# Sums of weight blocks made by adding transfers, and a seventh block product made from high and low digits

## The chip, the cores and the metric

The kernel runs on one core of a Trainium2 chip. The time is that of one execution on the device in microseconds, from the runs of the compiled program; the profile is that of one further execution.

## What is computed

256 tokens of width 1024 in float32 go through two layers of a first network and then through a tail of two more blocks. Each of the four has a mixer (sparse attention beside retention; stick-breaking attention beside a state-space model; attention over the best 64 keys) and an MLP with squared ReLU and 4096 hidden units. The change is in the four MLPs alone:

```python
# the two layers of the first network
h = rmsnorm(x, norm_mlp[i])
x = x + jnp.square(jax.nn.relu(h @ w_ff1[i])) @ w_ff2[i]
# the tail, MLPs "A." and "B."
return jnp.square(jax.nn.relu(x @ w1)) @ w2
```

## The kernel before

**Digits.** A float32 product on TensorE is replaced by three products of operands rounded to a shorter type: `products` multiplies low by high, high by low and high by high. ScalarE makes the high digits (a copy that rounds), VectorE the low ones (value minus high).

**Weights.** They come in tiles of 2 MB, loaded by SyncE (SP) into a ring of three slots. SP waits until TensorE has given back a slot (`tile_used`) and then issues the next load. In an MLP the tiles alternate: `ff1.n` holds 512 columns of the first matrix, `ff2.n` 512 rows of the second. The load of `ff2.n` goes to the slot of `ff1.n`, and so is issued when TensorE has finished with that.

**Seven products.** Of the eight `ff2` tiles the first seven (n = 0 to 6, `LAST` = 7) are not multiplied block by block (two token halves by two row halves by two column halves, eight products) but by a scheme with seven products. It needs sums of blocks of the hidden values (`dve_hidden_sums`, in `work`) and four sums of blocks of the weights: with b11, b12, b21, b22 the four blocks of a tile, `dve_form_sums` makes b22 - b12 into `t_sums[0]`, b12 - b11 in place in the ring's slot, b22 minus that into `t_sums[1]`, and b21 minus that into `t_sums[2]`. Six of the products are made by digits. The seventh, into bank 6, is the original float32 product of hidden values and `t_sums[2]`, two instructions of 512 columns a tile.

**One period**, the same for n = 2 to 7 in each MLP, on TensorE: unit (n, 0), which is eight times three products for each of two column blocks of `ff1.n` into bank 0; `seven_first(n-1)`, six products with the left columns' digits; unit (n, 1), again into bank 0; the slot of `ff1.n` is given back; `seven_second` and `seven_rest(n-1)`: left columns, bank 5 and bank 7 (right columns), bank 3 (`t_hi[0]`), bank 2 (`t_hi[1]`), bank 6. `form_used` counts four points of it: left columns' high digits read, right columns' read, bank 3 done, bank 2 done. Whoever writes into the buffers of the next tile waits for the count that frees them (`form_free`).

On ScalarE, in program order (`act_mlp_seven`): ReLU of unit (n, 0), square, high digits, half of `ff1.(n+1)`'s digits, ReLU of unit (n, 1) and the same again, digits of the hidden sums, then `act_column_forms(n)` and `act_right_forms(n)` for tile `ff2.n`, and after those the ReLU of unit (n+1, 0). For n = 1 this ReLU stands inside `act_right_forms` (`between`), behind the first cast. TensorE's unit (n+1, 1) waits for that ReLU, since it writes the same bank.

VectorE makes the low digits of `ff1` (`lower_columns`, L1294), the hidden sums and their low digits, the weight sums (L1400) and the forms' low digits (L1412). GpSimd works in the mixers and has nothing to do in the MLPs. `L527` is the line of the helper that issues every matmul.

## Time and profile before

| | |
|---|---|
| median of 3 runs | 1437.21 us (1435.92 to 1437.41) |
| the profiled execution's own time | 1436.92 us |
| its span, first to last instruction | 1435.1 us |
| TensorE busy | 1409.4 us, 98% |
| VectorE, ScalarE, GpSimd busy | 1093.2, 823.4, 286.9 us |
| granted TensorE clock, mean | 0.999 |
| DMA traffic | 250.28 MB, mean 174 GB/s |

Times in the rows below are microseconds from the start of the span unless marked ns. PE is TensorE's matmuls, PEld its weight loads, DVE VectorE, ACT ScalarE, POOL GpSimd, SP the engine that issues loads. Matmuls overlap, so the distance between the starts of two of them is what one costs, not its own duration. In brackets stands how long the engine was idle before an instruction and what ended that.

### The profile page before, as it was taken

How to read it: one execution, taken by the hardware profiler on the slowest of the kernel's cores; microseconds unless marked ns; L12 is line 12 of the kernel's file. 1: busy time of each engine (PE TensorE's matmuls, PEld its weight loads, DVE VectorE, ACT ScalarE, POOL GpSimd, SP SyncE). 2: the span in 40 equal slices, each digit the busy share in tenths (PEclk: the TensorE clock that was granted, in tenths of full speed). 3: DMA queues.
4: the chain of work that ended last, by engine and by line, in shares of the span. 5: the costliest groups of instructions: out<-in, count | busy, mean ns of one | idle time of the engine just before them, and what ended most of it. 6: DMA issues, size and time to landing. Idle time of an engine off the chain costs nothing.

```text
span 1435.1 us, 20256 instructions
## 1 busy us (share of the span) xinstructions
PE 1409.4 (98%) x8464; PEld 1186.1 (83%) x8464; DVE 1093.2 (76%) x1341; ACT 823.4 (57%) x1005; POOL 286.9 (20%) x109
## 2 busy tenths in 40 slices
PE   7999999999999999999999999999999999999997
PEld 5788889888877788888888788688888898888886
DVE  5335667989952455759999859878999887589998
ACT  4465636666445463637666446656666347277662
POOL 4598150000028695310000000000000005000000
PEclk9999999999999999999999999999999999999999
DMA  8933436555536632445656543406555453156551
GB/s 309 304 119 114 153 118 232 208 202 183 204 125 237 235 124 88 174 176 206 220 192 198 176 132 134 147 3 226 212 196 192 174 205 119 48 208 220 200 199 66
DMA packets 121226, 250.28 MB, mean 174 GB/s; under 512 B 15040, under 2 KB 27056, under 8 KB 121008
## 3 DMA queue, kind: packets, MB, share of 16 engines
q1 hardware_dynamic: 120872, 248.90, 49.5%
q8 instruction: 67, 1.10, 0.3%
q14 instruction: 23, 0.19, 0.0%
q10 hardware_dynamic: 264, 0.10, 0.0%
HBM read 247.94 MB, written 1.05 MB: 173 GB/s over the span
## 4 chain that ended last, share of the span: by engine, by line
PE 88%; DVE 6%; ACT 2%; POOL 1%; DMA 1%; issue 1%; DVEq 0%
PE psum L527 85%; PE psum L534 4%; POOL w_lo L1287 1%; DVE w_lo L1287 1%; DVE x L1481 1%; DMA ring<-in_w_ff 1%; DVE x L3031 1%; DVE big L3025 1%; DVE s_lo L1445 0%; DMA work<-in_norm_mix 0%; DVE rows L1791 0%; ACT work L1346 0%; ACT s_hi L1333 0%; ACT w_hi_rows L1267 0%; DVE tiny L3074 0%
## 5 line engine op out<-in xcount | busy, mean ns | idle before, releaser
L527 PE MATMUL psum<-ht_hi,w_lo 128*128 128x256 f32 x1008 | 292.9, 291 | 1.7 <-issue 1.0
L527 PE MATMUL psum<-w_lo,ht_hi 128*128 128x512 f32 (+1 forms) x576 | 222.3, 389 | 0.7 <-DVE w_lo L1287 0.7
L527 PEld LDWEIGHTS psum<-ht_hi,w_lo 128*128 128x128 f32 x1008 | 188.9, 187 | 11.5 <-issue 10.1
L527 PE MATMUL psum<-ht_lo,w_hi_tmp 128*128 128x256 f32 x464 | 129.5, 279 | 0.0
L527 PE MATMUL psum<-ht_lo,w_hi_rows 128*128 128x256 f32 x464 | 129.5, 279 | 0.0
L527 PE MATMUL psum<-ht_hi,w_hi_tmp 128*128 128x256 f32 x464 | 129.2, 279 | 0.0
L527 PE MATMUL psum<-ht_hi,w_hi_rows 128*128 128x256 f32 x464 | 129.2, 278 | 0.0
L527 PEld LDWEIGHTS psum<-w_lo,ht_hi 128*128 128x128 f32 x576 | 108.4, 188 | 21.9 <-DVE w_lo L1287 1.1
L1287 POOL TENSOR_TENSOR w_lo<-ring,w_hi_work 128x2048 fp32r<-128x2048 f32 x12 | 57.5, 4788 | 248.8 <-ACT w_hi_work L1267 248.8
L1314 ACT ACTIVATE w_hi_work<-ring 128x2048 fp32r<-128x2048 f32 x28 | 53.6, 1915 | 70.0 <-DMA ring<-in_w_ff 35.2
L527 PEld LDWEIGHTS psum<-ht_lo,w_hi_tmp 128*128 128x128 f32 x464 | 88.3, 190 | 5.8 <-issue 5.7
L527 PEld LDWEIGHTS psum<-ht_lo,w_hi_rows 128*128 128x128 f32 x464 | 88.2, 190 | 0.7
L527 PEld LDWEIGHTS psum<-ht_hi,w_hi_tmp 128*128 128x128 f32 x464 | 86.9, 187 | 0.0
L527 PEld LDWEIGHTS psum<-ht_hi,w_hi_rows 128*128 128x128 f32 x464 | 86.9, 187 | 0.0
L1287 POOL TENSOR_TENSOR w_lo<-ring,w_hi_big 128x2048 fp32r<-128x2048 f32 x3 | 13.7, 4567 | 348.9 <-DVE work L3025 348.9
L1346 ACT ACTIVATE work<-psum 128x512 f32<-128x512 f32 x60 | 35.6, 593 | 66.3 <-PE psum L527 66.3
L527 PE MATMUL psum<-hT,ring 128*128 128x256 f32 (+2 forms) x384 | 68.7, 337 | 0.0
L1600 ACT ACTIVATE big<-psum,tiny 128x512 f32<-128x512 f32 (+1 forms) x44 | 29.5, 671 | 67.9 <-PE psum L527 67.9
L527 PEld LDWEIGHTS psum<-hT,ring 128*128 128x128 f32 (+1 forms) x384 | 60.0, 184 | 7.6 <-issue 2.1
L1412 DVE TENSOR_TENSOR w_lo<-ring,w_hi_work 128x2048 fp32r<-128x2048 f32 x28 | 64.2, 2292 | 1.0
L1412 DVE TENSOR_TENSOR w_lo<-ring,w_hi_big 128x2048 fp32r<-128x2048 f32 x28 | 64.0, 2284 | 0.0
L1400 DVE TENSOR_TENSOR big<-ring 128x1024 f32<-128x1024 f32 x42 | 51.4, 1224 | 13.9 <-DMA ring<-in_w_ff 7.4
(451 smaller groups left out, 3955.5 us busy)
## 6 DMA issues: line engine op xcount, KB each, us to landing
ring<-in_w_ff SPq DMA_DIRECT2D x32, 2048.0 KB, 8.1
ring<-in_mlp_w SPq DMA_DIRECT2D x32, 2048.0 KB, 8.5
ring<-in_w_in SPq DMA_DIRECT2D x19, 2048.0 KB, 8.0
ring<-in_w_out SPq DMA_DIRECT2D x4, 2048.0 KB, 7.8
ring<-in_w_ple_gate SPq DMA_DIRECT2D x4, 2048.0 KB, 7.9
ring<-in_sb_ssm_w_in SPq DMA_DIRECT2D x4, 2048.0 KB, 8.4
ring<-in_dsa_w_in SPq DMA_DIRECT2D x3, 2048.0 KB, 8.0
ring<-in_w_up_nsa SPq DMA_DIRECT2D x2, 2048.0 KB, 7.9
```

Source lines behind the costliest of these rows:

```text
L527: ins = pe.matmul(o, lhsT, rhs, start=start, stop=stop)
L534: ins = pe.transpose(o, in_, ident[0:n, 0:n])
L1287: eng.tensor_tensor(w_lo[n % RING][:, c], ring[n % RING][:, c], w_hi[places[name][h]][:, 0:width].bitcast(F32), ALU.subtract) \
L1314: act.activation(col_hi, blocks(ring[at % RING][:, :])[:, :, :, 0:BANK], ACT.Copy).then_inc(st.up(form_hi), 1)
L1346: act.activation(h, b, ACT.Relu).then_inc(st.up(wide_.saved), 1)
L1400: dve.tensor_tensor(o, a, b, ALU.subtract).then_inc(st.up(t_summed), 1)
L1412: dve.tensor_tensor(low, v, hi.bitcast(F32), ALU.subtract).then_inc(st.up(form_lo), 1)
L1481: dve.scalar_tensor_tensor(out=o, in0=first, scalar=factor, in1=b if pre else o, op0=ALU.mult, op1=ALU.add) \
L1600: act.activation(z[:, t, c * BANK:c * BANK + m], b[:, 0:m], ACT.Copy, scale=nrr[:, t:t + 1]).then_inc(st.up(wide_.saved), 1)
L3025: return dve.tensor_tensor(o, a, b, op)
L3031: return dve.scalar_tensor_tensor(out=o, in0=a, scalar=s1, in1=b, op0=op0, op1=op1)
```

## The change

For the tiles n = 1 to 6 of each MLP (24 tiles) two of the four weight sums are no longer made by VectorE. SP loads such a tile in three pieces (`load_edges`): b12 and b22, 512 KB each, which raise `edge_in`, and then the left half, 1 MB. GpSimd's queue (`pool_form_sums`) issues three transfers of 512 KB a tile: a plain load of b22 into `t_sums[0]` once bank 3's products of the tile before are done (`corner_in`); once the edges are in, a transfer of b11 from the weights in HBM that adds to b12 in the ring's slot (`right_in`); and once the corner is in, one of b12 that adds to `t_sums[0]` (`third_in`). The signs are changed so that all of these are additions; the hidden sums and the end of the MLP (`dve_seven_products`) have the signs that go with it. ScalarE waits for `third_in` and `right_in` in place of VectorE's count. VectorE makes the other two sums (`dve_later_sums`) after `right_in`. Tile 0 keeps its four sums on VectorE.

The seventh product is made by digits in all 28 tiles: `DIGIT_SUMS` goes from 2 to 3, ScalarE casts a third sum, VectorE makes its low digits and those of the hidden block it is multiplied with (`dve_corner_low`), and TensorE does six products for two.

```diff
 SEVEN = ("", "A.", "B.")
-DIGIT_SUMS = 2
+DIGIT_SUMS = 3
 DIGIT_FORMS = 2 + DIGIT_SUMS
...
     s_sum = [work[:, 4096 + 2048 * n:5120 + 2048 * n] for n in range(2)]
-    S_WIDTH = 256 * DIGIT_FORMS
+    S_WIDTH = 256 * 4
     s_lo = [digits(f"s_lo{n}", "work", 4096 + 2048 * n, S_WIDTH)[:, :] for n in range(2)]
...
                             mm(o, hid_hi[:, s + 2 * u + v, 0:P], w[:, u, v, 0:BANK], False, final and u == 1 and v == 0)
-                sh, sl, sums_ = s_hi[n % 2], s_lo[n % 2], s_sum[n % 2]
+                sh, sl = s_hi[n % 2], s_lo[n % 2]
                 def by_digits(o, form, hi, low, stop, signal):
...
                 by_digits(bank[3], 1, t_hi[0], t_lows[pre][0], final, form_used)
-                if DIGIT_SUMS > 1:
-                    pe.wait_ge(form_lo.sem, st.at(form_lo, DIGIT_FORMS * m + 4))
-                    by_digits(bank[2], 3, t_hi[1], t_lows[pre][1], final, form_used)
-                else:
-                    pe.wait_ge(t_summed.sem, st.at(t_summed, 4 * m + 3))
-                    for u in range(2):
-                        mm(bank[2], s_form(sums_, 3, u), t_sums[pre][1][:, u, :], first and u == 0, final and u == 1,
-                           form_used if u == 1 else None)
-                pe.wait_ge(t_summed.sem, st.at(t_summed, 4 * m + 4))
+                pe.wait_ge(form_lo.sem, st.at(form_lo, DIGIT_FORMS * m + 4))
+                by_digits(bank[2], 3, t_hi[1], t_lows[pre][1], final, form_used)
+                pe.wait_ge(corner_low.sem, st.at(corner_low, m + 1))
+                pe.wait_ge(form_lo.sem, st.at(form_lo, DIGIT_FORMS * m + 5))
                 for u in range(2):
-                    mm(bank[6], hid_f[:, s + 2 * u + 1, P:S], t_sums[pre][2][:, u, :], first and u == 0, False)
+                    f = s + 2 * u + 1
+                    products(bank[6], hid_hi[:, f, P:S], hid_lo[:, f, P:S], t_hi[2][:, u, :], t_lows[pre][2][:, u, :],
+                             first and u == 0, False, None)
             def seven_open(n):
...
         at, m = tiles.index(f"{pre}ff2.{n}"), seventh(pre, n)
-        act.wait_ge(t_summed.sem, st.at(t_summed, 4 * m + 1))
+        if n:
+            act.wait_ge(third_in.sem, st.at(third_in, 16 * summed_nth(pre, n)))
+        else:
+            act.wait_ge(t_summed.sem, st.at(t_summed, 4 * m + 1))
         act.activation(t_hi[0], t_sums[pre][0], ACT.Copy).then_inc(st.up(form_hi), 1)
         form_free(st, act, tiles, pre, n, 2)
-        act.wait_ge(t_summed.sem, st.at(t_summed, 4 * m + 2))
+        if n:
+            act.wait_ge(right_in.sem, st.at(right_in, 16 * summed_nth(pre, n)))
+        else:
+            act.wait_ge(t_summed.sem, st.at(t_summed, 4 * m + 2))
         act.activation(right_hi, blocks(ring[at % RING][:, :])[:, :, :, BANK:D], ACT.Copy).then_inc(st.up(form_hi), 1)
-        if DIGIT_SUMS > 1:
-            act.wait_ge(t_summed.sem, st.at(t_summed, 4 * m + 3))
-            act.activation(t_hi[1], t_sums[pre][1], ACT.Copy).then_inc(st.up(form_hi), 1)
+        for i in range(1, DIGIT_SUMS):
+            act.wait_ge(t_summed.sem, st.at(t_summed, 4 * m + 2 + i))
+            act.activation(t_hi[i], t_sums[pre][i], ACT.Copy).then_inc(st.up(form_hi), 1)
     def act_hidden_forms(st, act, pre, n):
...
                 form_free(st, dve, tiles, pre, n, nth)
-            dve.tensor_tensor(o, a, b, ALU.subtract).then_inc(st.up(t_summed), 1)
+            dve.tensor_tensor(o, a, b, ALU.add).then_inc(st.up(t_summed), 1)
             dve.wait_ge(st.last.sem, st.reached())
+    def dve_later_sums(st, dve, tiles, pre, n):
+        at = tiles.index(f"{pre}ff2.{n}")
+        w = blocks(ring[at % RING][:, :])
+        b12, b21, b22 = w[:, :, 0, BANK:D], w[:, :, 1, 0:BANK], w[:, :, 1, BANK:D]
+        dve.wait_ge(tile_in[at % RING].sem, st.at(tile_in[at % RING], 16 * (at // RING + 1)))
+        dve.wait_ge(right_in.sem, st.at(right_in, 16 * summed_nth(pre, n)))
+        form_free(st, dve, tiles, pre, n, 4)
+        dve.tensor_tensor(t_sums[pre][1], b22, b12, ALU.add).then_inc(st.up(t_summed, 3), 3)
+        dve.wait_ge(st.last.sem, st.reached())
+        form_free(st, dve, tiles, pre, n, 5)
+        dve.tensor_tensor(t_sums[pre][2], b21, t_sums[pre][1], ALU.add).then_inc(st.up(t_summed), 1)
+        dve.wait_ge(st.last.sem, st.reached())
+    def pool_form_sums(st, pool, tiles, pre, n, matrix):
+        at, nth = tiles.index(f"{pre}ff2.{n}"), summed_nth(pre, n)
+        w, src = blocks(ring[at % RING][:, :]), matrix[n * BANK:(n + 1) * BANK, :].rearrange("(u v p) n -> p u v n", u=2, v=2)
+        form_free(st, pool, tiles, pre, n, 3)
+        pool.dma_start(t_sums[pre][0], src[:, :, 1, BANK:D]).then_inc(st.up(corner_in, 16), 16)
+        pool.wait_ge(edge_in.sem, st.at(edge_in, 32 * nth))
+        pool.dma_start(w[:, :, 0, BANK:D], src[:, :, 0, 0:BANK], accum_op=ALU.add).then_inc(st.up(right_in, 16), 16)
+        pool.wait_ge(corner_in.sem, st.at(corner_in, 16 * nth))
+        pool.dma_start(t_sums[pre][0], src[:, :, 0, BANK:D], accum_op=ALU.add).then_inc(st.up(third_in, 16), 16)
     def dve_form_lows(st, dve, tiles, pre, n, which):
         forms = [(1, lo[:, :, :, 0:BANK], w[:, :, :, 0:BANK], col_hi), (3, lo[:, :, :, BANK:D], w[:, :, :, BANK:D], right_hi)]
-        forms += [(2 * i + 2, t_lows[pre][i], t_sums[pre][i], t_hi[i]) for i in range(DIGIT_SUMS)]
+        forms += [((2, 4, 5)[i], t_lows[pre][i], t_sums[pre][i], t_hi[i]) for i in range(DIGIT_SUMS)]
         for i in which:
...
         dve.wait_ge(hid_hi_ready.sem, st.at(hid_hi_ready, FB // 2 * mlp_nth(pre) + 2 * n + 2))
-        dve.tensor_tensor(s1, a21, a22, ALU.add).then_inc(st.up(dve_step), 1)
+        dve.tensor_tensor(s1, a21, a22, ALU.subtract).then_inc(st.up(dve_step), 1)
         dve.tensor_tensor(s3, a11, a21, ALU.subtract).then_inc(st.up(dve_step), 1)
         dve.wait_ge(st.last.sem, st.reached())
-        dve.tensor_tensor(s4, a12, s2, ALU.subtract).then_inc(st.up(s_summed), 1)
+        dve.tensor_tensor(s4, a12, s2, ALU.add).then_inc(st.up(s_summed), 1)
         dve.wait_ge(st.last.sem, st.reached())
...
         dve.tensor_tensor(lo, h, hi.bitcast(F32), ALU.subtract).then_inc(st.up(hid_lo_ready, 2), 2)
+    def dve_corner_low(st, dve, pre, n):
+        s = 4 * (n % 2)
+        hi, lo, h = (v[:, s:s + 4, P:S].rearrange("p (u v) t -> p u v t", v=2)[:, :, 1] for v in (hid_hi, hid_lo, hid_f))
+        dve.wait_ge(s_summed.sem, st.at(s_summed, seventh(pre, n) + 1))
+        dve.tensor_tensor(lo, h, hi.bitcast(F32), ALU.subtract).then_inc(st.up(corner_low), 1)
     def dve_hidden_low(st, dve, pre, f):
...
         dve_hidden_sums_low(st, dve, pre, 0)
+        dve_corner_low(st, dve, pre, 0)
         dve_form_lows(st, dve, tiles, pre, 0, range(3, DIGIT_FORMS))
...
             dve_hidden_sums_low(st, dve, pre, n)
-            dve_form_sums(st, dve, tiles, pre, n)
+            dve_corner_low(st, dve, pre, n)
+            dve_later_sums(st, dve, tiles, pre, n)
             dve_form_lows(st, dve, tiles, pre, n, range(DIGIT_FORMS))
...
         half = [[x[:, t, c * BANK:(c + 1) * BANK] for c in range(2)] for t in range(TT)]
-        def added(t, c, b, signal=dve_step):
+        def added(t, c, b, signal=dve_step, sign=nrr):
             o = half[t][c]
-            factor, first = (nrr[:, t:t + 1], b) if not pre else (ALPHA, o)
+            factor, first = (sign[:, t:t + 1], b) if not pre else (ALPHA, o)
             dve.scalar_tensor_tensor(out=o, in0=first, scalar=factor, in1=b if pre else o, op0=ALU.mult, op1=ALU.add) \
             if pre:
-                dve.tensor_tensor(half[t][c], half[t][c], y_sums[pre], ALU.add).then_inc(st.up(dve_step), 1)
+                dve.tensor_tensor(half[t][c], half[t][c], y_sums[pre], ALU.subtract if c else ALU.add).then_inc(st.up(dve_step), 1)
             else:
-                added(t, c, y_sums[pre])
+                added(t, c, y_sums[pre], sign=nrr_less if c else nrr)
         def summed(b):
             dve.wait_ge(st.last.sem, st.reached())
+        if not pre:
+            dve.tensor_scalar(nrr_less, nrr, -1.0, None, ALU.mult).then_inc(st.up(dve_step), 1)
         used = 4 * seventh(pre, LAST - 1)
...
             lower_split(st, pool, TILES, SPLITS, name)
+        for n in range(1, LAST):
+            pool_form_sums(st, pool, TILES, "", n, I["w_ff2"][st.where.layer])
     CH = 4
...
         return [v[:, 4 * half:4 * half + 4, t * P:(t + 1) * P] for v in (hT, ht_hi, ht_lo)]
+    def summed_ahead(name):
+        _, _, num = name.rpartition("ff2.")
+        return num.isdigit() and 1 <= int(num) < LAST
+    def load_edges(sp, place, src):
+        halves = [v.rearrange("p (u v) n -> p u v n", v=2) for v in (place, src)]
+        for v in range(2):
+            sp.dma_start(*(h[:, :, v, BANK:D] for h in halves)).then_inc(edge_in.sem, 16)
+        return [h[:, :, 0:BANK] for h in (place, src)]
     def load_parameters(sp, tile_):
...
         pool.wait_ge(form_used.sem, DEPTH * form_used.per_layer)
-        for v in (b4, magtab[:, :, 0:1]):
-            pool.memset(v, 0.0).then_inc(st.up(zeroed), 1)
+        pool.memset(b4, 0.0).then_inc(st.up(zeroed), 1)
+        pool.wait_ge(tile_used.sem, (DEPTH - 1) * tile_used.per_layer + TILES.index(f"ff2.{LAST - 1}") + 1 + RING)
+        pool.memset(magtab[:, :, 0:1], 0.0).then_inc(st.up(zeroed), 1)
         pool.wait_ge(ple_added.sem, st.at(ple_added, 0))
         pool.memset(states[:, :, :, 0:1].rearrange("p r j k -> p (r j) k"), 0.0).then_inc(st.up(zeroed), 1)
+        for n in range(1, LAST):
+            pool_form_sums(st, pool, TILES2, "A.", n, I["mlp_w2_2"][0])
         pool.wait_ge(masked.sem, st.at(masked, 2))
             lower_split(st, pool, TILES2, SPLITS2, name)
+        for n in range(1, LAST):
+            pool_form_sums(st, pool, TILES2, "B.", n, I["mlp_w2_2"][1])
     def small_loads(i):
...
                 place, s = w_tile(n, (k, m)), s.rearrange("(k p) n -> p k n", p=P)
+                if summed_ahead(name):
+                    place, s = load_edges(sp, place, s)
                 if n == i == 0:
```

## Rows read from the trace of the kernel before

**Rows 1.** The profile's page: busy time by engine, and the chain by engine.

```profile
PE 1409.4 (98%) x8464; PEld 1186.1 (83%) x8464; DVE 1093.2 (76%) x1341; ACT 823.4 (57%) x1005; POOL 286.9 (20%) x109
...
PE 88%; DVE 6%; ACT 2%; POOL 1%; DMA 1%; issue 1%; DVEq 0%
```

**Rows 2.** Windows, one period of MLP A: window, time, busy us by engine.

```profile
1050.70:1072.12 21.42, 21.42 (x138) 18.81 (x137) 19.68 (x17) 14.36 (x14) 0.00 (x0) 1.00 0.56 197
```

**Rows 3.** Timeline of PE around the seventh product: start us, us, instruction.

```profile
1049.38 1.88 PE L527 MATMUL psum<-big,work 128*128 128x512 f32 x4
1050.70 0.68 PE L527 MATMUL psum<-ht_hi,w_lo 128*128 128x256 f32 x1
1051.22 0.28 PE L527 MATMUL psum<-ht_lo,w_hi_tmp 128*128 128x256 f32 x1
```

**Rows 4.** Lines of PE by form: the seventh product in the layers' MLPs.

```profile
L527 PE MATMUL psum<-hT,work 128*128 128x512 f32 x56 | 26.3, 592 | 0.0
```

**Rows 5.** Timeline of PE: last product of the third form, and what follows.

```profile
1069.16 0.40 PE L527 MATMUL psum<-t_hi,s_hi 128*128 128x512 f32 x1
...
1070.80 1.88 PE L527 MATMUL psum<-big,work 128*128 128x512 f32 x4
...
1079.55 0.28 PE L527 MATMUL psum<-ht_hi,w_lo 128*128 128x256 f32 x1
```

**Rows 6.** Timeline of ACT over the same stretch.

```profile
1071.95 1.92 ACT L1314 ACTIVATE w_hi_work<-ring 128x2048 fp32r<-128x2048 f32 x1 [3.24 <-DMA ring<-in_mlp_w]
1073.77 1.04 ACT L1320 ACTIVATE t_hi<-big 128x1024 fp32r<-128x1024 f32 x1
1074.72 1.90 ACT L1325 ACTIVATE w_hi_big<-ring 128x2048 fp32r<-128x2048 f32 x1
1076.52 1.05 ACT L1328 ACTIVATE t_hi<-big 128x1024 fp32r<-128x1024 f32 x1
1078.36 0.60 ACT L1346 ACTIVATE work<-psum 128x512 f32<-128x512 f32 x1 [0.80 <-PE psum L527]
```

**Rows 7.** Timeline of PE, first period of that MLP: the same two places.

```profile
1004.89 0.39 PE L527 MATMUL psum<-t_hi,s_hi 128*128 128x512 f32 x1
...
1015.29 0.28 PE L527 MATMUL psum<-ht_hi,w_lo 128*128 128x256 f32 x1
```

**Rows 8.** The tile's load at 1064.2 us: its issue on SP, its landing.

```profile
L2326 SPq DMA_DIRECT2D ring<-in_mlp_w x1: 368/368/368, 1064.2 to 1064.2; - x1
...
DMA to landing us min/median/max: 7.7/7.7/7.7
```

**Rows 9.** DMA issues: tile<-source, queue, count, size, median us to landing.

```profile
ring<-in_mlp_w SPq DMA_DIRECT2D x32, 2048.0 KB, 8.5
...
big<-in_w_ple SPq DMA_DIRECT2D x2, 1024.0 KB, 4.9
...
const<-in_ln_mix_b SPq DMA_DIRECT2D x2, 512.0 KB, 10.2
...
out<-x SPq DMA_DIRECT2D x4, 256.0 KB, 2.1
```

**Rows 10.** Timeline of DVE over the same stretch as rows 6.

```profile
1071.95 1.23 DVE L1400 TENSOR_TENSOR big<-ring 128x1024 f32<-128x1024 f32 x1 [0.21 <-DMA ring<-in_mlp_w]
...
1087.36 0.43 DVE L1420 TENSOR_TENSOR work<-work 128x256 f32<-128x256 f32 x1 [1.40 <-ACT hid_hi L1353]
```

**Rows 11.** Timeline of PE at the span's start, with its longest idle time.

```profile
6.30 0.56 PE L527 MATMUL psum<-const,work 8*128 8x8 f32 x2 [6.30 <-DMA work<-in_norm_mix]
...
9.68 1.91 PE L527 MATMUL psum<-x,const 128*128 128x512 f32 x2
```

**Rows 12.** Lines of PE: another product of the shape seen at 9.68 us.

```profile
L527 PE MATMUL psum<-big,pT 128*128 128x512 f32 x32 | 14.4, 592 | 0.0
```

**Rows 13.** Timeline of PE around its second longest idle time.

```profile
917.59 1.90 PE L527 MATMUL psum<-tmp,const 128*128 128x384 f32 x8
922.16 2.00 PE L527 MATMUL psum<-tmp,const 128*128 128x384 f32 x8 [2.67 <-DVE rows L3025]
```

More of the change, by code:

```diff
@@ L430, in program @@
     nss, nrr = tiny[:, 168:170], tiny[:, 170:172]
+    nrr_less = tiny[:, 174:176]
     kss, krr = tiny[:, 172:173], tiny[:, 173:174]
@@ L444, in program @@
     aux = Line(bank[2:4], AUX, sig("aux_ready", len(AUX)), sig("aux_saved", len(AUX), 2))
-    act_step, dve_step, pool_step = sig("act_step", 62), sig("dve_step", 65 + 3 * LAST + 8), sig("pool_step", 23)
+    act_step, dve_step, pool_step = sig("act_step", 62), sig("dve_step", 66 + 3 * LAST + 8), sig("pool_step", 23)
     norm_ready = sig("norm_ready", 1)
@@ L481, in program @@
     t_summed, form_hi, form_lo = sig("t_summed", 4 * LAST), sig("form_hi", DIGIT_FORMS * LAST), sig("form_lo", DIGIT_FORMS * LAST)
+    corner_in, right_in, third_in = (sig(name, 16 * (LAST - 1)) for name in ("corner_in", "right_in", "third_in"))
+    edge_in = sig("edge_in", 32 * (LAST - 1))
     s_summed, s_high, s_low = sig("s_summed", LAST), sig("s_high", LAST), sig("s_low", LAST)
+    corner_low = sig("corner_low", LAST)
     form_used, seven_read, y_copied = sig("form_used", 4 * LAST), sig("seven_read", 1), sig("y_copied", 1)
@@ L503, in mlp_nth, with summed_nth @@
         return 1 if pre == "B." else 0
+    def summed_nth(pre, n):
+        return (LAST - 1) * mlp_nth(pre) + n
     def seventh(pre, n):
@@ L2325, in sp_tail @@
                 s = w[:, c * BANK:c * BANK + m]
-            sp.dma_start(w_tile(n, (k, m)), s.rearrange("(k p) n -> p k n", p=P)) \
-                .then_inc(tile_in[n % RING].sem, 16)
+            place, s = w_tile(n, (k, m)), s.rearrange("(k p) n -> p k n", p=P)
+            if summed_ahead(name):
+                place, s = load_edges(sp, place, s)
+            sp.dma_start(place, s).then_inc(tile_in[n % RING].sem, 16)
             if name == "sb2":
@@ L3549, in _ @@
                 place, s = w_tile(n, (k, m)), s.rearrange("(k p) n -> p k n", p=P)
+                if summed_ahead(name):
+                    place, s = load_edges(sp, place, s)
                 if n == i == 0:
```

## The prediction

> **What bounds the kernel now.** I read the page first: TensorE is busy 98% of the span and holds 88% of the chain that ended last [rows 1]. So nothing is won except by giving TensorE less to do, and anything that makes it wait is paid in full. Then the stretch of one period of an MLP by windows: in 21.42 us TensorE is busy for all 21.42 at granted clock 1.00, VectorE for 19.68, ScalarE for 14.36, GpSimd for nothing, and the DMA engines for a share of 0.56 [rows 2]. TensorE is the limit and the others are hidden under it, but not by much. How much is not in the shares; it is in the timelines of ScalarE and TensorE, and there one wait decides.
>
> Call F the moment at which PE ends the third form's products (bank 3), 1069.16 + 0.40 = 1069.56 us [rows 5]. From F to the first product of the next period's second unit, 1079.55, PE runs 10.0 us without a gap. That second unit writes bank 0 again, so it needs the ReLU (L1346) of the first unit. ScalarE runs in order, and before this ReLU stand the casts of the *previous* tile: columns, t_hi, right half, t_hi [rows 6]. They start when the tile lands (1071.95), end at 1077.6, and ScalarE is then idle for only 0.80 us until the unit's result is there. The ReLU ends at 1078.96 and PE needs it at 1079.55. So there are about 1.4 us of slack between the casts and a stall of TensorE.
>
> **TensorE's gain.** The two float32 products of the seventh block are four records. From the first (1049.38) to the second product of the next unit (1051.22) is 1.84 us [rows 3]. By digits they become six products. Seven digit products start between 1069.16 and 1070.80, 0.234 us each [rows 5]; six and the unit's first product (half as wide, so about 0.12) make 1.41 + 0.12 = 1.53 us. That saves 0.31 us. There are 28 such pairs: 56 records of the layers' two MLPs are 14 pairs, the tail's two MLPs have 14 more [rows 4]. Fully on the path this is 28 x 0.31 = 8.7 us.
>
> **VectorE, ScalarE, SP.** VectorE loses two of four sums a tile (1.23 us each) [rows 10], gains one low half of 1.2 us and a corner of 256 columns (0.43 us, as the operation of that size at 1087.36) [rows 10]: 0.8 us less in each later tile, hidden, since TensorE is the limit. It now also waits for the second adding transfer, with the low halves queued behind it; the first of these is there two sums and one low half (2.5 + 2.3 us) after the landing, and PE needs it when the second unit ends, at F + 21.4 - 5.4 = F + 16 [rows 2, 8]. A landing up to F + 11 is free, and a stall of PE moves the need back too. ScalarE gains a cast of 1.0 us a tile, in front of that ReLU [rows 6]. In each MLP's first tile this is the only cost; between 0 and 4 x 1.0 us reach PE, I take 1. SP issues three loads instead of one, 2 x 0.37 us more [rows 8], covered by ScalarE's longer wait below. The negated factor, the changed signs and the moved memsets lie off the path: nothing.
>
> **The new chain.** For six of seven tiles, t_hi's cast waits for third_in, and third_in is the end of two transfers in a row on GpSimd's queue: the corner's load cannot be issued before F (form_used, third count: PE still reads this buffer), and the adding transfer waits for the load to land. Before, VectorE did this in 1.2 us. Call Y the time from F until third_in. After it ScalarE still has to do t_hi, right half and two more casts, then the ReLU: by steps of rows 6, 0.95 + 1.80 + 1.0 + 1.0 + 0.60, with two hand-overs 5.4 us. PE stalls for Y + 5.4 - 10.0 = Y - 4.6. In the first of the six the ReLU stands right behind the t_hi cast (`between`), so it is Y + 0.95 + 0.60 + 0.1 - 10.0 = Y - 8.35; the 10.0 is the same there (1005.28 to 1015.29) [rows 7]. Behind the stalled unit stand the rest of the period and the next F, so nothing gives the time back: next period's loads start from the new F. The stalls sum to 4 x (5 (Y - 4.6) + (Y - 8.35)) = 24 Y - 125.4.
> The gain of 0.31 lies between F and the stalled unit, so it only shortens time that the stall fills; it counts once per MLP, after the last F: 1.2 us. With the 1 us of above the sum is 24 Y - 125.6.
>
> **How long is Y?** No transfer of GpSimd and no adding one is in this trace, so I bound it. Loads: 2 MB land in 8.5 (this tile: 7.7), 1 MB in 4.9, a store of 256 KB in 2.1 us, and 512 KB behind a tile on the same queue in 10.2 [rows 8, 9]. From 1 and 2 MB with 8.0 as the middle: 3.1 us a MB and 1.8 fixed. 512 KB alone: 3.35 us, by the store nearer 3.0. Two in a row: Y = 6.0 at the least. Above: twice 10.2, Y = 20. Between them I look at what is in flight. At F the tile issued 5.4 us before still has 2.3 us of data to land; the corner shares the engines with it and lands in 1.8 + 2 x 1.55 = 4.9. The adding transfer starts at F + 4.9, beside the next tile's load (issued F + 3.2), and behind what is left of the other adding transfer: 4.9 + 0.7 = 5.6. So Y = 10.5, and the stalls are 24 x 10.5 - 125.6 = 126 us.
> The Trainium skill (DMA: Bandwidth & Descriptors, "Anatomy of one DMA — SWDGE (gpsimd) path") gives a fit for a transfer from this queue, 2.0 us plus bytes over 436 GB/s, an estimate of 3.2 us here; by that alone the kernel would take about 1473 us. No run here shows it yet.
>
> **What the stall does to the clock.** Stalls would be 5.9 us. The only idle time of that size is at the start of the span, 6.3 us [rows 11]. After it two float32 products of 128x512 take 1057 ns each, where the same shape takes 592 later [rows 12]: the time is that of the 1.2 GHz level although the page lists 1.00. An idle time of 2.67 us costs nothing that shows (eight products take 2.00 us after, 1.90 before) [rows 13]. At half rate from 6.30 to about 11.6 us the loss is some 2.7 us. I add it to the 20 long stalls: 54 us; the lower bound is 0, since PE came cold into the span anyway.
> The skill (TensorE: Matmul & The Clock Gate, Part 1) says that an idle TensorE falls back to the lower level; by it the 54 us belong in the sum, without it the forecast is 1563.
> Sum, against the profiled execution's own 1436.9 us (span 1435.1, median of the runs 1437.2): 1436.9 + 126 + 54 = 1617.
>
> **Rivals.**
> (a) The transfers run nearly alone, Y = 6 to 8.3, and the clock holds. DMA share 0.56 speaks for it, two more transfers in flight at that very moment against. Y = 6: 20 x 1.4 = 28, 1465; Y = 8.3: 20 x 3.7 = 74, 1511.
> (b) Adding is slow, or GpSimd is late in starting transfers. An adding transfer must read and write its target; at twice the time for data in it and in the one before it, Y = 14: 24 x 14 - 125.6 + 54 = 264, 1701; more is open above. The skill (SBUF — State Buffer, "SBUF: two separate sides") has GpSimd kept from writing descriptors while VectorE runs in certain copy modes; VectorE's instructions here are two-input subtractions, so I give it no weight of its own.
> (c) Faster: both transfers land before ScalarE is due, Y under 4.6. Then no stall remains and the 8.7 us of TensorE count in full: 1428. For it speaks that 256 KB can land in 2.1 us; against it that two of 512 KB would each have to land in 2.3. It decides at Y = 4.6 in the five later tiles.
> (d) The change moves the wait but nets out: Y = 4.6 to 5.0 in effect, within 0.2% (what a measurement of this kernel can tell from no change).
>
> **How the numbers follow.** Main case, Y from 8.3 to 13.5 with or without the loss of clock, 1511 to 1690: 0.60, value 1617. (a) 0.15, (b) 0.13, (c) 0.08, (d) 0.04. Range 1490 to 1710: the main case, the upper part of (a), the lower part of (b). Chances: faster 0.08, same 0.04, slower 0.88.
>
> **What would show it.** PE waiting in 24 places, in front of the second unit of tiles 2 to 7 of every MLP, released by ACT L1346 work; ScalarE waiting before t_hi for a DMA from the ff2 weights; corner's load issued at F; periods of 27 to 30 us instead of 21.4; six digit products where two float32 stood. If ScalarE's t_hi cast starts under 4.6 us after F, I am wrong in sign; if the products behind a stall keep 0.117 us a step, the 54 us are wrong.

## The result and the profile after

| | before | after |
|---|---|---|
| median of 4 runs each, in turn on one chip | 1437.04 us (1435.92 to 1437.41) | 1737.62 us (1731.56 to 1739.38) |
| ratio, 95% interval | | 1.209 (1.207 to 1.210) |
| span of the profiled execution | 1435.1 us | 1735.2 us |
| granted TensorE clock, mean | 0.999 | 0.923 |

The kernel is 300 us slower; the forecast was 180 slower, at most 273. The page of after, whose first rows answer to [rows 1]:

```profile
span 1735.2 us, 20552 instructions
...
PE 1458.7 (84%) x8520; PEld 1247.4 (72%) x8520; DVE 1073.9 (62%) x1351; ACT 846.3 (49%) x1033; POOL 363.2 (21%) x181
...
PEclk9999998888899999988788999997887999988888
...
q0 software_dynamic: 16512, 37.75, 10.7%
...
PE 60%; DMA 21%; ACT 8%; DVE 6%; issue 3%; POOL 1%; DVEq 0%; SPq 0%; ACTq 0%; POOLq 0%
```

TensorE is no longer the limit: 84% busy instead of 98%, and the DMA engines, 1% of the chain before, hold 21%. The waits of after (who waited <- for whom: us in all, times, longest) say where the 300 us are:

```profile
PE psum L535 <- ACT work L1357: 250.3, 26, 13.7
ACT t_hi L1328 <- DMA big<-in_w_ff: 125.8, 12, 12.0
ACT t_hi L1328 <- DMA big<-in_mlp_w: 120.9, 12, 11.9
```

TensorE waits 250.3 us for the ReLU (now L1357), where it waited 0.3 before, and is busy 49.3 us longer (1458.7 - 1409.4). The two make 299.3 of the span's 300.1 us; nothing else of size changed. Of the 26 waits 24 are of 6.5 to 13.7 us, the other two of 0.84. The two rows of ScalarE are the 24 casts of `t_hi[0]`, each behind a transfer into the sums' buffer. To see one of them, take the period that starts with F at 1256.44 + 0.40 = 1256.84 us. GpSimd's timeline (start, duration of the issue, idle before):

```profile
1257.15 0.75 POOL L1433 DMA_DIRECT2D big<-in_mlp_w  x1 [28.05 <-PE psum L535]
1257.89 1.24 POOL L1435 DMA_DIRECT2D ring<-in_mlp_w  x1
1261.59 1.20 POOL L1437 DMA_DIRECT2D big<-in_mlp_w  x1 [2.45 <-DMA big<-in_mlp_w]
```

ScalarE's timeline, which answers to [rows 6]:

```profile
1271.45 1.06 ACT L1328 ACTIVATE t_hi<-big 128x1024 fp32r<-128x1024 f32 x1 [10.03 <-DMA big<-in_mlp_w]
1272.41 1.89 ACT L1336 ACTIVATE w_hi_big<-ring 128x2048 fp32r<-128x2048 f32 x1
1274.21 1.99 ACT L1339 ACTIVATE t_hi<-big 128x1024 fp32r<-128x1024 f32 x2
1276.10 0.57 ACT L1357 ACTIVATE work<-psum 128x512 f32<-128x512 f32 x1
```

TensorE's timeline, the products of bank 3, of the seventh block product and of the two units, which answers to [rows 3, 5]:

```profile
1256.44 0.40 PE L535 MATMUL psum<-t_hi,s_hi 128*128 128x512 f32 x1
...
1258.08 0.40 PE L535 MATMUL psum<-t_hi,hid_lo 128*128 128x512 f32 x1
...
1259.26 0.39 PE L535 MATMUL psum<-t_hi,hid_hi 128*128 128x512 f32 x1
1259.49 0.28 PE L535 MATMUL psum<-ht_hi,w_lo 128*128 128x256 f32 x1
...
1266.31 0.40 PE L535 MATMUL psum<-w_hi_work,hid_hi 128*128 128x512 f32 x1
1276.82 0.55 PE L535 MATMUL psum<-ht_hi,w_lo 128*128 128x256 f32 x1 [10.12 <-ACT work L1357]
1277.17 0.41 PE L535 MATMUL psum<-ht_lo,w_hi_rows 128*128 128x256 f32 x1
1277.39 0.41 PE L535 MATMUL psum<-ht_hi,w_hi_rows 128*128 128x256 f32 x1
```

Read together: the corner's load is issued 0.3 us after F and the third transfer 4.4 us later, when the corner has landed. `third_in` comes 9.9 us after that, and the cast starts at 1271.45, so Y = 14.6. The ReLU follows behind three more casts, and TensorE, done at 1266.7, stands for 10.12 us. Y - 4.6 is 10.0. The seventh product is there as forecast: six starts from 1258.08 to 1259.26, and 1.41 us until the next unit. F comes again after 33.9 us, where a period was 21.4.

The clock is in the windows (as [rows 2]; the column after POOL is the granted clock):

```profile
1276.70:1280.00 3.30, 3.18 (x15) 3.21 (x16) 3.30 (x4) 3.06 (x3) 0.00 (x0) 0.50 0.00 0
1280.00:1284.00 4.00, 4.00 (x28) 4.00 (x28) 2.23 (x2) 0.00 (x0) 0.00 (x0) 0.74 0.01 4
1284.00:1292.00 8.00, 8.00 (x41) 6.62 (x40) 4.77 (x7) 4.68 (x5) 0.99 (x2) 1.00 0.69 241
```

After the idle 10 us the granted clock is 0.50, the 1.2 GHz level, then mixed, and 1.00 from 1284. The products of 128x256 are 0.21 us apart in the first stretch and 0.117 in full clock.

### The profile page after: what moved, and what is told of

It reads as the page before. It is cut to its first block, busy times and chain, and to the rows that moved or that the text cites. A ratio compares the mean times of both kernels' runs of the same rounds, so it can differ in the third digit from the quotient of the medians.

```text
span 1735.2 us, 20552 instructions
## 1 busy us (share of the span) xinstructions
PE 1458.7 (84%) x8520; PEld 1247.4 (72%) x8520; DVE 1073.9 (62%) x1351; ACT 846.3 (49%) x1033; POOL 363.2 (21%) x181
## 4 chain that ended last, share of the span: by engine, by line
PE 60%; DMA 21%; ACT 8%; DVE 6%; issue 3%; POOL 1%; DVEq 0%; SPq 0%; ACTq 0%; POOLq 0%
PE psum L535 57%; DMA big<-in_w_ff 10%; DMA big<-in_mlp_w 10%; PE psum L542 3%; ACT t_hi L1339 3%; ACT w_hi_big L1336 3%; DVE w_lo L1292 1%; POOL w_lo L1292 1%; ACT work L1357 1%; DVE x L1526 1%; DVE x L3094 0%; DVE big L3088 0%; DMA ring<-in_mlp_w 0%; DVE s_lo L1488 0%; DMA work<-in_norm_mix 0%
## 5 line engine op out<-in xcount | busy, mean ns | idle before, releaser
L535 PE MATMUL psum<-ht_hi,w_lo 128*128 128x256 f32 x1008 | 311.3, 309 | 251.4 <-ACT work L1357 250.3
L535 PEld LDWEIGHTS psum<-ht_hi,w_lo 128*128 128x128 f32 x1008 | 215.5, 214 | 264.3 <-issue 260.9
L535 PE MATMUL psum<-ht_lo,w_hi_rows 128*128 128x256 f32 x464 | 153.3, 330 | 0.0
L535 PE MATMUL psum<-ht_hi,w_hi_rows 128*128 128x256 f32 x464 | 152.3, 328 | 0.0
L1328 ACT ACTIVATE t_hi<-big 128x1024 fp32r<-128x1024 f32 x28 | 29.6, 1056 | 247.2 <-DMA big<-in_w_ff 125.8
L535 PEld LDWEIGHTS psum<-ht_lo,w_hi_rows 128*128 128x128 f32 x464 | 114.1, 246 | 0.0
L535 PEld LDWEIGHTS psum<-ht_hi,w_hi_rows 128*128 128x128 f32 x464 | 111.8, 241 | 0.0
L1357 ACT ACTIVATE work<-psum 128x512 f32<-128x512 f32 x60 | 35.2, 586 | 114.9 <-PE psum L535 114.9
L1433 POOL DMA_DIRECT2D big<-in_w_ff x12 | 9.2, 766 | 376.1 <-PE psum L535 376.1
L1292 POOL TENSOR_TENSOR w_lo<-ring,w_hi_work 128x2048 fp32r<-128x2048 f32 x12 | 57.5, 4788 | 99.8 <-ACT w_hi_work L1272 99.8
L1422 DVE TENSOR_TENSOR hT<-ring 128x1024 f32<-128x1024 f32 x12 | 14.7, 1225 | 89.8 <-DMA ring<-in_w_ff 89.8
L1422 DVE TENSOR_TENSOR big<-ring 128x1024 f32<-128x1024 f32 x12 | 14.7, 1225 | 86.6 <-DMA ring<-in_mlp_w 86.6
## 6 DMA issues: line engine op xcount, KB each, us to landing
ring<-in_w_ff SPq DMA_DIRECT2D x20, 2048.0 KB, 13.7
ring<-in_mlp_w SPq DMA_DIRECT2D x20, 2048.0 KB, 13.3
```

The source lines that it names most:

```text
L535: ins = pe.matmul(o, lhsT, rhs, start=start, stop=stop)
L1292: eng.tensor_tensor(w_lo[n % RING][:, c], ring[n % RING][:, c], w_hi[places[name][h]][:, 0:width].bitcast(F32), ALU.subtract) \
L1328: act.activation(t_hi[0], t_sums[pre][0], ACT.Copy).then_inc(st.up(form_hi), 1)
L1357: act.activation(h, b, ACT.Relu).then_inc(st.up(wide_.saved), 1)
L1422: dve.tensor_tensor(t_sums[pre][1], b22, b12, ALU.add).then_inc(st.up(t_summed, 3), 3)
L1433: pool.dma_start(t_sums[pre][0], src[:, :, 1, BANK:D]).then_inc(st.up(corner_in, 16), 16)
```

## The experiments

All times are medians; the kernel before gave 1436.4 to 1437.5 beside them. e1, e2, e4, e6, e8, e10 and e11 have two runs each, the others four to eight. Where the diffs below say nothing else, they are against the kernel after; `...` marks what is left out.

**How long the transfers take, and what makes them long.** Four kernels vary them.

e1, the third transfer plain, and e2, both plain (the kernels leave out these sums and compute another result, but everything waits as before):

```diff
-pool.dma_start(w[:, :, 0, BANK:D], src[:, :, 0, 0:BANK], accum_op=ALU.add).then_inc(st.up(right_in, 16), 16)
+pool.dma_start(w[:, :, 0, BANK:D], src[:, :, 0, 0:BANK]).then_inc(st.up(right_in, 16), 16)          # e2
...
-pool.dma_start(t_sums[pre][0], src[:, :, 0, BANK:D], accum_op=ALU.add).then_inc(st.up(third_in, 16), 16)
+pool.dma_start(t_sums[pre][0], src[:, :, 0, BANK:D]).then_inc(st.up(third_in, 16), 16)              # e1 and e2
```

> The last of the three transfers loads b12 instead of adding it (the sum is left out of the computation, everything waits as before). Theory A, adding itself is what makes it long (9.8 us from issue to landing, where the plain one of the same size takes 4.1 beside the same traffic): it lands 3 us or more sooner, 24 x 3 = 72 us off the stalls, 1665 us or less. Theory B, the share of the DMA engines taken by the next tile's load (2 MB, issued 3 us after F): it still takes 9 us or more, and the kernel stays above 1710.

> Neither GpSimd transfer adds (two sums are left out of the computation). Theory A: the right one falls from 9.1 to some 5 us as well, third to 5, F to third_in is about 9.5 us, stalls 24 x 9.5 - 125 = 103 us and less loss of clock: 1560 to 1600. Theory B: above 1700.

e6, the right half's sum back on VectorE, in place, one transfer fewer in flight. SP also loads the tile in one piece again, not in three:

```diff
-pool.dma_start(w[:, :, 0, BANK:D], src[:, :, 0, 0:BANK], accum_op=ALU.add).then_inc(st.up(right_in, 16), 16)
+dve.tensor_tensor(b12, b12, w[:, :, 0, 0:BANK], ALU.add).then_inc(st.up(t_summed, 2), 2)
...
-        return num.isdigit() and 1 <= int(num) < LAST        # summed_ahead
+        return False
```

> Of the three GpSimd transfers the one that adds to the right half is gone, VectorE makes that sum as before; corner and third stay. Theory A (the third's own adding, and SP's load beside it): third still takes 9 us or more, 1715 to 1740 us. Rival (it queues behind the other adding transfer, as the prediction had it with 0.7 us): third under 8 us, 1690 or less.

e8, SP's next load of 2 MB held back until the third transfer has landed:

```diff
             sp.wait_ge(tile_used.sem, where.value(tile_used, n + 1))
+            hold_back(sp, where, name)   # ff1.n+2 (and ff2.7): sp.wait_ge(third_in of ff2.n)
```

> The changed kernel with SP's next load of 2 MB held back until third_in, so that the third transfer has the DMA engines nearly to itself. If the engines' sharing makes up what adding does not (adding took 2.3 us by the run with a plain third: 9.8 against 7.5), the third takes 6 to 7 us instead of 10.2, F to third_in about 11; the time depends on what the late load delays: 1650 to 1720. If the length is the transfer's own, it stays at 9 us or more and the kernel is slower than 1737.

From issue to landing (min/median/max of 24), after: corner, right half, third.

```profile
DMA to landing us min/median/max: 4.0/4.3/5.4
...
DMA to landing us min/median/max: 6.9/9.2/10.7
...
DMA to landing us min/median/max: 9.4/10.2/11.8
```

The third in e1:

```profile
DMA to landing us min/median/max: 6.8/7.5/9.4
```

The same in e8:

```profile
DMA to landing us min/median/max: 5.6/6.3/7.4
```

| kernel | time | ratio | third, median | TensorE's wait for the ReLU |
|---|---|---|---|---|
| after | 1737.6 | 1.209 | 10.2 | 250.3 |
| e1 third plain | 1667.7 | 1.161 (1.158 to 1.163) | 7.5 | 184.8 |
| e2 both plain | 1667.8 | 1.161 (1.156 to 1.165) | 7.5 | 185.8 |
| e6 right on VectorE | 1716.3 | 1.194 (1.192 to 1.197) | 9.5 | 228.8 |
| e8 load held back | 1640.8 | 1.142 (1.140 to 1.144) | 6.3 | 156.5 |

Adding costs 2.7 us of the third transfer's 10.2 (e1, just short of theory A) and the right half's adding nothing that the time shows (e2, a miss: its landing fell from 8.7 to 5.4 and the third's stayed at 7.5). The right half's transfer beside it is worth 0.7 (e6, as theory A had it). The largest part is the load of 2 MB that SP issues in those microseconds: held back, the adding transfer takes 6.3 instead of 10.2 (e8: the landing as expected, the time 9 us below the expected range). The parts are not to be added up: what adding costs without that load, no run shows. The times follow Y: e1's third is 2.7 us shorter, 24 x 2.7 = 65, and the wait fell by 65.5. The other side pays too: SP's 2 MB loads in the MLPs take 13.3 to 13.7 us in after, against 8.1 (the layers) and 8.5 (the tail, [rows 9]) before, and 7.9 and 8.5 in e8.

**Which half of the change costs.** e3 has the digits and every sum on VectorE; e4 the transfers and the float32 seventh product.

```diff
-            pool_form_sums(st, pool, TILES, "", n, I["w_ff2"][st.where.layer])   # e3: no transfers,
...
-            dve_later_sums(st, dve, tiles, pre, n)
+            dve_form_sums(st, dve, tiles, pre, n)                                # four sums on VectorE
...
-DIGIT_SUMS = 3
+DIGIT_SUMS = 2                                                                   # e4
...
-                    products(bank[6], hid_hi[:, f, P:S], hid_lo[:, f, P:S], t_hi[2][:, u, :], t_lows[pre][2][:, u, :],
-                             first and u == 0, False, None)
+                    mm(bank[6], hid_f[:, s + 2 * u + 1, P:S], t_sums[pre][2][:, u, :], first and u == 0, False)
```

> The seventh product by digits, all four sums on VectorE, no GpSimd transfer. Theory: without the stall TensorE's 8.7 us show in part, since VectorE now has 19.7 + 1.2 + 0.4 = 21.3 us of work in a period of 21.1: 1429 to 1435 us. Rival: VectorE becomes the limit and ScalarE's extra cast reaches the ReLU: 1438 to 1450. Whoever thinks that the digits have a part in the 300 us expects more than 1450.

> The adding transfers with the seventh product in float32. Theory: the transfers make the whole loss and the extra cast of 1.0 us stands in front of the ReLU in 20 periods, so 1737 - 20 = 1717 us (1705 to 1725). Rival, the digits carry a good part of it: under 1690.

e4: 1717.3 us as expected, 1.195 (1.193 to 1.198), waits for the ReLU of 227.6: the transfers make nearly all of the loss. e3: 1457.6, 1.015 (1.013 to 1.017), above the ranges of its theory and its rival: the digits too have a part in the 300 us, some 20. VectorE's and ScalarE's timelines of e3 where tile 2 of an MLP lands (at 1041.9, by ScalarE's first cast of it):

```profile
1043.40 1.22 DVE L1482 TENSOR_TENSOR s_lo<-work,s_hi 128x1024 fp32r<-128x1024 f32 x1
1044.54 0.42 DVE L1470 TENSOR_TENSOR hid_lo<-work,hid_hi 128x256 fp32r<-128x256 f32 x1
1044.88 1.22 DVE L1405 TENSOR_TENSOR big<-ring 128x1024 f32<-128x1024 f32 x1
```

```profile
1041.94 1.92 ACT L1319 ACTIVATE w_hi_work<-ring 128x2048 fp32r<-128x2048 f32 x1 [0.35 <-DMA ring<-in_mlp_w]
1046.13 1.06 ACT L1325 ACTIVATE t_hi<-big 128x1024 fp32r<-128x1024 f32 x1 [2.26 <-DVE big L1405]
```

and TensorE's and the window behind it:

```profile
1051.88 0.55 PE L535 MATMUL psum<-ht_hi,w_lo 128*128 128x256 f32 x1 [3.77 <-ACT work L1351]
```

```profile
1051.80:1056.00 4.20, 4.12 (x22) 4.16 (x23) 4.20 (x4) 3.03 (x3) 0.00 (x0) 0.59 0.00 0
```

VectorE takes up the tile 3 us late, behind its own low halves, and the ReLU comes so much later that TensorE waits 3.77 us and then runs at 0.59 of its clock.

**Moving the ReLU.** If the ReLU's place behind the cast is the link, taking it out must break the chain. e5 is after with the next unit's ReLU ahead of the cast that waits for `third_in`; e7 is e3 with it behind the right half's cast.

```diff
-            act_right_forms(st, act, tiles, pre, n)
+            act_right_forms(st, act, tiles, pre, n, lambda: relu(2 * n + 2))
...
         at, m = tiles.index(f"{pre}ff2.{n}"), seventh(pre, n)
+        if between:
+            between()                            # e5: first of all; e7: after right_hi's cast
...
-            if n > 2:
-                relu(2 * n)                      # it stood here, behind the tile's last cast
```

> The changed kernel with ScalarE's ReLU of the next unit ahead of the casts that wait for third_in. Theory (the loss is the ReLU standing behind the transfers, not the transfers as such): PE no longer waits for the ReLU; third_in at F + 14.6, then 2.75 us of casts and 2.3 us of VectorE give the right half's low digits at F + 19.7, where PE wants them at F + 17.0: 2.7 us in 24 periods, no loss of clock, about 1500 us (1480 to 1530). Rival: the transfers' load on the DMA engines or another reader of the late sums holds the kernel back anyway: over 1600.

> Digits only, sums on VectorE, with the ReLU ahead of the last two casts. Theory 1 (in the run with digits only the waits of 3.8 us came from the ReLU behind the third cast while VectorE was late with the sums): they go, 1429 to 1436 us, a little better than before. Theory 2 (VectorE itself is the limit): the stall comes back as a wait for low digits, 1440 to 1460.

e5: 1576.7 us, 1.099 (1.096 to 1.102), 161 better than after. The waits for the ReLU are gone (1.7 us); in their place TensorE waits for the right half's low digits, which VectorE makes behind the same late cast. The sum of these waits, one of them, and the windows behind it:

```profile
PE psum L535 <- DVE w_lo L1446: 92.3, 27, 5.0
...
1176.28 0.77 PE L535 MATMUL psum<-w_hi_big,s_lo 128*128 128x512 f32 x1 [3.06 <-DVE w_lo L1446]
```

```profile
1176.00:1180.00 4.00, 3.72 (x9) 2.99 (x10) 4.00 (x5) 3.90 (x6) 0.00 (x0) 0.50 0.80 300
1180.00:1184.00 4.00, 4.00 (x15) 3.17 (x14) 3.84 (x6) 2.94 (x3) 0.26 (x1) 0.72 0.00 0
1184.00:1192.00 8.00, 8.00 (x60) 7.54 (x59) 3.79 (x4) 2.30 (x3) 2.92 (x3) 1.00 0.86 215
```

The single wait was forecast (2.7 us, 3.06 found), the sum was not, and the time lies between the theory's range and the rival's: 92.3 us in 27 waits instead of 24 x 2.7 = 65, and behind most of them the clock falls. Of the 24 waits of 2.8 to 5.0 us, 21 have a granted clock of 0.50 to 0.65 in the 4 us that follow, and three (of 3.07, 3.50 and 3.60 us) have 1.00. This is the window behind the one of 3.07:

```profile
378.18:382.18 4.00, 4.00 (x17) 3.27 (x18) 4.00 (x4) 3.94 (x5) 0.00 (x0) 1.00 0.74 277
```

So TensorE's busy time stays at 1448.1.

e7: 1446.1 us, 1.006 (1.005 to 1.007). Waits for the ReLU fell from 17.9 to 9.3 us, and they are still for the ReLU, not for low digits as theory 2 had it. Four of them, one in tile 2 of each MLP, are of 1.9 us. The windows behind the first and the third:

```profile
285.56:289.56 4.00, 4.00 (x21) 4.00 (x22) 4.00 (x2) 3.97 (x5) 0.00 (x0) 0.58 0.00 0
1044.96:1048.96 4.00, 4.00 (x34) 4.00 (x35) 4.00 (x2) 3.97 (x5) 0.00 (x0) 1.00 0.00 0
```

**Starting the corner a period earlier.** In the tail's MLPs e10 and e11 give the first sum two places, so that its transfers need not wait for F, and send the third before the right half's. e10 is otherwise after, e11 is e5.

```diff
-        form_free(st, pool, tiles, pre, n, 3)
+        form_free(st, pool, tiles, pre, n - 1, 3)     # MLPs A and B: freed one period earlier
+    other_sum = big[:, 6656:7680]                     # where tiles with odd n have the first sum
```

> The changed kernel, but MLPs A and B keep the first sum in two places by turns, so that corner and third are under way long before F, and the right half's transfer comes after them. Theory (the loss is a chain of two transfers that starts at F): in A and B only the right half's transfer is left, landing about 7 us after F, stalls of some 2 us in 12 tiles instead of 10; the layers keep their 150 us: about 1610 (1590 to 1640). Rival (the DMA engines' load or queue holds them, wherever they start): over 1680.

> The same with the ReLU ahead of the casts in all four MLPs. The layers lose 70 us as in the run with the ReLU first (half of its 140), A and B nothing or a few us: about 1510 (1495 to 1530). Where the transfers cost something by themselves, A and B lose more than 30 us.

e10: 1611.8 us, 1.122 (1.120 to 1.124), as expected (1610); waits 143.2 instead of 250.3. Twelve of the 24 chains no longer start at F and the time falls by 126 of the 300 us. e11: 1529.4, 1.064 (1.062 to 1.066), 20 us above the value that was expected and at the upper end of its range. MLPs A and B were to lose nothing or a few us, and each has one long wait, in tile 1. There the third transfer, the right half's and the next tile's corner are issued within 1.5 us (1083.8 to 1085.2 in MLP A), and the right half's lands only at 1098.8, before VectorE can make the low digits that TensorE waits for:

```profile
1103.75 2.08 PE L542 MATMUL psum<-w_lo,hid_hi 128*128 128x512 f32 x4 [6.91 <-DVE w_lo L1468]
```

The other is of 7.1 us, and the granted clock behind each is 0.50.

**The sum on GpSimd itself.** e9 is e7 with the first weight sum of tiles 1 to 6 by a GpSimd instruction.

```diff
+        pool.tensor_tensor(t_sums[pre][0], w[:, :, 1, BANK:D], w[:, :, 0, BANK:D], ALU.add)
```

> Digits only with the moved ReLU, and the first of the four sums of tiles 1 to 6 made by GpSimd from the tile in the ring (a subtraction of 128x1024, some 2.4 us by its 4.6 us for 2048 columns), not by VectorE. Theory (VectorE, with 21.3 us of work in a period of 21.1, was what held the digits back): VectorE has 20.0 us, and TensorE's gain shows: 1428 to 1434 us. Rival: GpSimd's sum comes late, or slows VectorE beside it, and the kernel stays at 1440 or more.

e9: 1466.6 us, 1.021 (1.020 to 1.022), slower than e7 by 20.6. The groups of its instructions, and one place where the two engines meet, show why the relief did not come:

```profile
L1436 POOL TENSOR_TENSOR big<-ring 128x1024 f32<-128x1024 f32 x24 | 74.9, 3120 | 728.2 <-DMA ring<-in_mlp_w 430.2 <-DMA ring<-in_w_ff 298.0
L1487 DVE TENSOR_TENSOR s_lo<-work,s_hi 128x1024 fp32r<-128x1024 f32 x28 | 60.6, 2165 | 6.2 <-ACT s_hi L1344 6.2
...
278.74 4.34 POOL L1436 TENSOR_TENSOR big<-ring 128x1024 f32<-128x1024 f32 x1 [20.51 <-DMA ring<-in_w_ff]
...
280.74 3.42 DVE L1487 TENSOR_TENSOR s_lo<-work,s_hi 128x1024 fp32r<-128x1024 f32 x1
```

GpSimd takes 3.12 us for what VectorE does in 1.23. The 2165 ns of VectorE's low half are a mean of two kinds: 1.22 us, as before, where no sum of GpSimd runs beside it, and 3.42 where one does. In other tiles it is a smaller instruction that meets the sum (0.42 becomes 2.6 us). 23 of the 24 sums cost VectorE 2.2 us in this way, more than the 1.2 that they save it; its busy time rises from 1126.2 (e7) to 1156.2 us.

**What the digit products are worth, and where they pay.** e12 is the *kernel before* with bank 6's two float32 products replaced by six digit products of operands that exist already; the right operands of the seventh product are left out.

```diff
+                    by_digits(bank[6], 3, t_hi[1], t_lows[pre][1], False, None)
                     by_digits(bank[2], 3, t_hi[1], t_lows[pre][1], final, form_used)
...
-                    mm(bank[6], hid_f[:, s + 2 * u + 1, P:S], t_sums[pre][2][:, u, :], first and u == 0, False)
```

> The kernel before, but bank 6 gets six digit products of operands that are there already (t_hi[1], its low digits and the fourth hidden sum), so the seventh product is wrong and costs no cast and no subtraction: what is left out is the right operand of that product. It measures TensorE's gain alone: 28 x 0.31 = 8.7 us by the prediction, 1428.4 us (1427 to 1430). If the switch between the two kinds of product costs something besides, more; if VectorE is what TensorE waits for, nothing: 1436 or more.

e12: 1431.6 us, 0.996 (0.995 to 0.998), 5.3 to 5.9 us gained, less than the 8.7 expected. Its page:

```profile
PE 1401.2 (98%) x8520; PEld 1196.0 (84%) x8520; DVE 1088.7 (76%) x1341; ACT 823.5 (58%) x1005; POOL 286.8 (20%) x109
```

TensorE is busy 8.2 us less (1409.4 - 1401.2), 0.29 a product and nearly the forecast, but idle 2.9 us more. Why then does e7 lose? Its four waits of 1.9 us are in tile 2, and TensorE is busy 5.4 us longer than in e12 for the same number of products, at a mean granted clock of 0.996. In e7 two full periods by windows:

```profile
1087.07:1108.17 21.10, 21.10 (x139) 19.20 (x138) 20.80 (x18) 14.97 (x15) 0.00 (x0) 1.00 0.56 198
1108.17:1129.26 21.09, 21.09 (x139) 19.16 (x139) 20.80 (x18) 14.98 (x15) 0.00 (x0) 1.00 0.54 205
```

Against [rows 2] the period is 0.32 us shorter, as it should be, but VectorE is busy for 20.80 of it instead of 19.68. What is left, 0.3 us, works off hardly any backlog, and VectorE has one early: in MLP A its first sum of tile 2 starts 3.3 us after ScalarE's first cast of that tile (1.3 in the kernel before), and in tiles 3 to 6 it still starts 1.8 to 2.1 us after (0.0 before). e13 and e14 are e7 with the digits only from tile 3 and from tile 2.

```diff
+DIGITS_FROM = 3                                  # e14: 2
...
+                if n < DIGITS_FROM:
+                    pe.wait_ge(t_summed.sem, st.at(t_summed, 4 * m + 4))
+                    for u in range(2):
+                        mm(bank[6], hid_f[:, s + 2 * u + 1, P:S], t_sums[pre][2][:, u, :], first and u == 0, False)
+                    return
```

> All sums on VectorE, no transfers, the ReLU of the next unit behind the right half's cast (as in e7), and the seventh product by digits only from tile 3 of each MLP; tiles 0 to 2 keep the float32 product. Theory (VectorE is late only in the first tiles, where in e7 the t_hi cast of tile 2 starts 3.8 us later than before; from tile 3 its 20.8 of 21.1 us a period are hidden): the waits for L1353's work go back from 9.3 us to under 3, and 16 of 28 tiles keep their part of the 5.6 us that the digit products gave alone, 3.2 us: 1434 us, ratio 0.998. Rival (VectorE is too full in every tile): 16 of 28 parts of what e7 loses, 5 us, so 1442.

> As e13, with the digits from tile 2 of each MLP. Theory (late only in tiles 1 and 2): tile 2 gains 0.2 us in TensorE and, entering with less of a backlog than in e7, loses at most the 1.5 us by which tile 2 fell back there: between 1433 (nothing lost) and 1439 us. Rival (too full everywhere): 20 of 28 parts of e7's loss, 1443.

e13: 1433.1 us (1432.4 to 1435.3), 0.9976 (0.9965 to 0.9986). e14: 1434.0 (1432.0 to 1434.9), 0.9974 (0.9964 to 0.9985). Both came out as their theories had it. They are faster than the kernel before by 3 to 4 us, a small gain, but clear of the interval, and e13's page has TensorE back in the chain:

```profile
PE 1403.6 (98%) x8496; PEld 1191.9 (83%) x8496; DVE 1114.6 (78%) x1375; ACT 836.9 (58%) x1021; POOL 287.0 (20%) x109
...
PE 87%; DVE 9%; POOL 1%; ACT 1%; DMA 1%; issue 1%; DVEq 0%
```

In MLP A of e13 VectorE's first sum of tile 2 is again 1.3 us behind. So VectorE is too late only in the first tiles, and the digits pay behind them; whether tile 2 gains or loses a little is below what the two runs tell apart.

## Why the prediction was wrong in size

**The mechanism held.** 24 stalls of TensorE in front of the second unit, released by the ReLU behind a cast that waits for `third_in`; the corner issued at F; and a stall of Y - 4.6 (10.0 by the formula, 10.12 in the trace). Over all 24 the cast starts 15.1 us after the corner's issue on average, and that is 0.3 us after F, so Y is 15.4. The prediction's sum with that, 24 x 15.4 - 125.4 = 244, is 6 from the 250.3 measured. e10, which takes the start at F away from twelve chains, and e5, which takes the ReLU from behind the cast, confirm both ends of the chain.

**The step that failed is the length of Y, 10.5 against 15.4.** 24 x 4.9 = 118 us, of the 121 by which the forecast missed. The corner was right: 4.9 forecast, 4.3 to its landing (the median) and 4.8 to the third's issue (the average). The third transfer was put at 5.6, "beside the next tile's load", and took 10.2. Its 5.6 were 3.35 for 512 KB alone, 1.55 for sharing with the load, as for the corner, and 0.7 for the other transfer. Without the load the third is shorter by 3.9 (e8), so sharing was the larger error; adding, for which the main case charged nothing, is 2.7 (e1). Two rows show the sharing, the first of after, while its transfers are in flight, the second of the kernel before, while one load of 2 MB is: the DMA engines are full in both.

```profile
1263.00:1267.00 4.00, 3.70 (x26) 3.09 (x24) 0.00 (x0) 0.00 (x0) 0.00 (x0) 1.00 1.04 300
...
1066.00:1070.00 4.00, 4.00 (x19) 3.22 (x18) 3.84 (x6) 2.71 (x2) 0.00 (x0) 1.00 0.99 392
```

The prediction let a mean share of 0.56 over the period speak for rival (a), with little loss by sharing. That mean holds stretches in which one load alone fills the engines. The Trainium skill's fit (DMA: Bandwidth & Descriptors, "Anatomy of one DMA — SWDGE (gpsimd) path"), 3.2 us for this size as an estimate, is below all 72 transfers of after, the least of which took 4.0; here the measurement decides. Rival (b), "adding is slow", was at Y = 14 and 1701, and the run lies beyond it; it was given 0.13, and the range ended at its lower part.

**The clock was right.** 54 us forecast. TensorE's busy time is 1458.7 against 1401.2 in e12, which has as many products at a granted clock of 0.999: 57.5 us. The forecast took 2.7 us for each of 20 stalls of 5.9 us, and the stalls were 24 of 10.4 us on average; but e8, whose stalls are 6.4 us on average, loses 54.0 us (1455.2), so the size did not hang on the longer stalls. The rule of the Trainium skill cited for it (TensorE: Matmul & The Clock Gate, Part 1, an idle TensorE falls back) agrees with the windows, 0.50 after 10 us idle.

**TensorE's gain.** That the stalls swallow it was right. Its size, 0.31 us for each of 28, was not tested by after, but by e12: 0.29 us each in TensorE's busy time, of which 0.20 each, 5.6 in all, reach the time. In a full period it is 0.32 (e7, 21.10 against 21.42).

**What was hidden at no cost.** VectorE's own net was put at 0.8 us less in each of 24 tiles, and its instructions bear that out: two sums of 1.22 us fewer, a low half of 1.22 and a corner of 0.42 more. That the busy time fell by 19.3 us (1093.2 to 1073.9), which is 24 x 0.8, is chance: tile 0 of each MLP has 1.6 us more, and four small instructions outside the change take 5.0 us less. Without its transfers the digits add 1.1 us (20.80 against 19.68), and with them the cast of 1 us stands before the ReLU: from 1.4 us of slack, that is some 20 us (e3). The 1 us taken for it was a guess that after could not show.

**What stays open.** Of the third transfer's 10.2 us no run has the part that adding takes by itself, since none has it plain with the load held back. Why waits of one length are followed by either level of the clock is not shown. A load held back together with the moved ReLU and the second place for the sum was not tried.

## What to carry to other kernels

Ask of a transfer that replaces an instruction when it can start and who waits for its landing: here two in a row could start only at F, and 1.2 us of VectorE became 15.4. Size it by what is in flight in those very microseconds, from the timeline, not by a mean share of the DMA engines. An in-order engine passes such a wait on to all behind it, so first move what is urgent (the ReLU) ahead of it; and give a full engine more work only in the stretches in which it has caught up (e13).
